# Sums of squares added on VectorE, a constant tile run through TensorE during the first load, and the first eight experts of the first group looked up early

## The reference, cut to what matters

```
y = rmsnorm(h, mix_norm_g[0]);  h = h + mixer_ab(y)         # attention heads and short convolutions
y = rmsnorm(h, ffn_norm_g[i]);  h = h + peer(y)             # both layers
...
rmsnorm: x * rsqrt(mean(x*x) + EPS) * g
peer:    q = y @ w_q                                        # 8 heads x 2 halves x 128
         s = q . sub_keys (128 keys for each half)
         val, idx = top_k(s, 16)                            # for each half
         cand = val0[:, None] + val1[None, :]               # 16 x 16
         top_val, top_pos = top_k(cand, 16);  expert = idx0*128 + idx1 at top_pos
         out = sum_k softmax(top_val)_k * gelu(u[expert_k] . y) * v[expert_k]
```

## Time and profile before

| | |
|---|---|
| median of 3 runs | 1607.42 us (1606.4 to 1611.76) |
| the profiled execution's own time | 1606.77 us |
| its span | 1605.0 us |
| busy: PE, DVE, ACT, POOL | 1046.8, 1111.9, 461.3, 500.8 us |
| DMA | 646.70 MB, mean 403 GB/s |

### The profile page before, as it was taken

How to read it: one execution, slowest core, us unless ns; L and a number is a source line. 1 busy time by engine, 2 the same in 40 slices (tenths; PEclk the granted TensorE clock), 3 DMA queues, 4 the chain that set the end, 5 groups by cost and what they waited for, 6 DMA issues and landing times.

```text
span 1605.0 us, 19986 instructions
## 1 busy us (share of the span) xinstructions
PE 1046.8 (65%) x6936; PEld 711.0 (44%) x6936; DVE 1111.9 (69%) x3119; ACT 461.3 (29%) x953; POOL 500.8 (31%) x541
## 2 busy tenths in 40 slices
PE   8997876757734577778574477877576444544454
PEld 8995642525511266656362155665263111211111
DVE  3436878676457776997756777987765777777764
ACT  4111553111111345742111335743222111111110
POOL 0003333333223333332322323332332333333330
PEclk9998877867955699888796589877788555555666
DMA  9979999999999999999999999999999999999994
GB/s 369 408 259 402 374 420 421 417 421 420 416 420 420 421 378 415 420 415 394 422 416 420 421 411 403 417 405 374 420 418 419 421 422 421 421 421 423 420 420 190
DMA packets 105300, 646.70 MB, mean 403 GB/s; under 512 B 11632, under 2 KB 15728, under 8 KB 37616
## 3 DMA queue, kind: packets, MB, share of 16 engines
q0 software_dynamic: 76032, 553.68, 83.5%
q1 hardware_dynamic: 25536, 89.66, 14.2%
q10 hardware_dynamic: 3632, 2.08, 0.4%
HBM read 644.33 MB, written 1.05 MB: 402 GB/s over the span
## 4 chain that ended last, share of the span: by engine, by line
DMA 40%; PE 28%; DVE 15%; POOL 5%; issue 5%; ACT 4%; DVEq 2%; POOLq 0%; ACTq 0%
DMA ring<-in_uv_dram,expert 36%; PE ps L691 14%; DVE ring L1221 7%; PE ps L868 7%; POOL ring L406 5%; DMA wring<-in_wall_dram 5%; PE ps L881 2%; DVE side L1276 2%; PE ps L698 1%; PE ps L909 1%; ACT side L590 1%; PE ps L856 1%; ACT yg L471 1%; ACT osb L651 1%; ACT L475 0%
## 5 line engine op out<-in xcount | busy, mean ns | idle before, releaser
L1221 DVE CUSTOM_DVE_ANT_0 ring<-ring,ps 128x1024 f32<-128x1024 f32 x528 | 634.8, 1217 | 314.9 <-DMA ring<-in_uv_dram,expert 261.2
L406 POOL DMA_INDIRECT ring<-in_uv_dram,expert x528 | 498.7, 945 | 1068.8 <-PE ps L868 808.2
L868 PE MATMUL ps<-ring,mix 128*32 128x512 f32 x2112 | 369.3, 834 | 327.3 <-DVE mix L1237 327.3
L868 PEld LDWEIGHTS ps<-ring,mix 128*32 128x32 f32 x2112 | 67.8, 135 | 531.7 <-DVE mix L1237 391.0
L665 ACT ACTIVATE gel<-dots 128x4 f32<-128x4 f32 x132 | 27.1, 205 | 761.7 <-DVE dots L1221 761.4
L691 PE MATMUL ps<-yT,wring 128*128 128x128 f32 (+1 forms) x1184 | 159.6, 294 | 48.2 <-DMA wring<-in_wall_dram 27.6
L691 PEld LDWEIGHTS ps<-yT,wring 128*128 128x128 f32 x1184 | 150.7, 202 | 63.6 <-DMA wring<-in_wall_dram 34.2
L881 PE MATMUL ps<-sel,osb 128*128 128x16 f32 x528 | 84.1, 304 | 70.6 <-ACT osb L651 70.6
L881 PEld LDWEIGHTS ps<-sel,osb 128*128 128x128 f32 x528 | 80.7, 241 | 108.9 <-ACT osb L651 108.9
L590 ACT ACTIVATE side<-ident,params 128x128 f32<-128x128 f32 x310 | 96.3, 389 | 15.6 <-PE ps L909 14.8
L856 PE MATMUL ps<-ident,yg 128*128 128x128 f32 x264 | 48.0, 342 | 58.0 <-DVE dots L1221 58.0
(11 more groups left out here) (211 smaller groups left out, 1135.5 us busy)
## 6 DMA issues: line engine op xcount, KB each, us to landing
wring<-in_wall_dram SPq DMA_DIRECT2D x102, 512.0 KB, 11.8
ring<-in_wall_dram SPq DMA_DIRECT2D x44, 512.0 KB, 14.5
kept<-in_wall_dram SPq DMA_DIRECT2D x24, 512.0 KB, 17.0
ring<-in_uv_dram,expert POOLq DMA_INDIRECT x528, 16.1
out_dram<-fo ACTq DMA_DIRECT2D x16, 64.0 KB, 6.7
hT<-in_xT_dram ACTq DMA_DIRECT2D x1, 576.0 KB, 15.9
hT<-in_xT_dram SPq DMA_DIRECT2D x2, 256.0 KB, 3.2
params<-in_smalls_dram ACTq DMA_DIRECT2D x1, 380.0 KB, 17.7
```

The costliest lines, as they stand in the source:

```text
L406: pool.indirect_dma_start(out=ring[:, i % R, :], out_offset=None, in_=uv, in_offset=bass.IndirectOffsetOnAxis(ap=expert[:, n % 2, k:k + 1] ...
L868: mm = pe.matmul(po[32 * j:32 * j + 32, half, :], mix[:, k, :], ring[:, slot, D + 512 * half:D + 512 * (half + 1)], start=(q == 0), stop=( ...
L1221: nc.vector.tensor_tensor_reduce(out=row, in0=row, in1=yrep, scale=1.0, scalar=0.0, op0=ALU.mult, op1=ALU.add, accum_out=dots[:, k:k + 1]) ...
```

## The change

1. *Sums of squares.* VectorE adds the eight squared blocks (one reduction each for part A and xB, seven additions for the second sum), and TensorE needs one matmul with ones in place of eight. The first one stands behind `inA` 0. The reduction of xB stands in VectorE's program behind the evacuation of `inA` 4.
2. *A constant tile.* Before `inA` 0, TensorE runs eight matmuls of `ones` by `ones` into a bank that nobody reads. ScalarE runs a root on the constant `epsc` before it waits for the first sum.
3. *Order on ScalarE.* The loads of xB and of the parameters are issued behind the root of the first norm.
4. *Experts.* The blocks of `qA` (and `qB`) go by halves: blocks 0 to 7 are the first half of all heads. Half 0 of group 0's scores is made after `qA` 9, and VectorE picks its best 16 after the evacuation of `qA` 11. The first eight experts of group 0 are finished, and announced by `s_half`, before the other eight.

```
 [ScalarE]
+            act.wait_ge(s_const, 6)
+            act.activation(warm[:, :], epsc[:, :], ACT.Sqrt)
+            act.wait_ge(s_ss, 1)
+            act.activation(rstd[:, 0:TA], ps[:, 7, 0:TA], ACT.Sqrt, bias=epsc[:, :], scale=1.0 / D).then_inc(s_rms, 1)
             act.dma_start(hT[:, :, TA:L], xT[:, C * TA:C * L].rearrange("p (c t) -> p c t", t=TB)).then_inc(s_x[2], 16)
             act.dma_start(params[:, PAR["conv"]:NPAR], smalls[:, PAR["conv"]:NPAR]).then_inc(s_par2, 16)
-            act.wait_ge(s_const, 6)
-            act.wait_ge(s_ss, 1)
-            act.activation(rstd[:, 0:TA], ps[:, 7, 0:TA], ACT.Sqrt, bias=epsc[:, :], scale=1.0 / D).then_inc(s_rms, 1)
             act.wait_ge(s_x[2], 16)
             act.activation(sqB0[:, :, :], hT[:, :, TA:L], ACT.Square).then_inc(s_sqx, 1)
...
 [TensorE]
             pe.wait_ge(s_const, 6)
-            for c in range(C):
-                pe.wait_ge(s_sq, 2 * c // C + 1)
-                last = pe.matmul(ps[:, 7, 0:TA], ones[:, :], sq[:, c, :], start=(c == 0), stop=(c == C - 1))
-            last.then_inc(s_ss, 1)
+            for _ in range(8):
+                pe.matmul(ps[:, 6, 0:P], ones[:, :], ones[:, :], start=True, stop=True)
             for k in range(24):
                 if k == 0:
                     pe.wait_ge(s_hg, C)
                 chunk("inA", k, lambda c: yT[:, c, 0:TA], TA)
+                if k == 0:
+                    pe.wait_ge(s_sum, 1)
+                    pe.matmul(ps[:, 7, 0:TA], ones[:, :], rs[:, 0:TA], start=True, stop=True).then_inc(s_ss, 1)
...
-            pe.wait_ge(s_sqx, 1)
+            pe.wait_ge(s_sumx, 1)
             pe.wait_ge(s_ze, 2)
-            for c in range(C):
-                last = pe.matmul(ps[:, 3, 0:TB], ones[:, :], sqB0[:, c, :], start=(c == 0), stop=(c == C - 1))
-            last.then_inc(s_ssx, 1)
+            pe.matmul(ps[:, 3, 0:TB], ones[:, :], xs[:, 0:TB], start=True, stop=True).then_inc(s_ssx, 1)
...
             for k in range(C):
                 chunk("outA", k, lambda c: mixT[:, c, 0:TA], TA)
-                if k >= 2:
-                    second_sums(k - 2)
...
                 chunk("qA", k, lambda c: hg2[:, c, :], TA)
                 if k == 0:
-                    second_sums(C - 2)
-                    second_sums(C - 1)
+                    pe.wait_ge(s_sum, 2)
+                    pe.matmul(ps[:, 7, 0:TA], ones[:, :], rs[:, 0:TA], start=True, stop=True).then_inc(s_ss, 1)
+                if k == 9:
+                    evacuated(pe, "qA", 6)
+                    evacuated(pe, "qA", 7)
+                    pe.wait_ge(s_par2, 16)
+                    score(0, 0).then_inc(s_sc0, 1)
...
 [VectorE]
+            dve.wait_ge(s_sq, 2)
+            nc.vector.tensor_reduce(out=rs[:, 0:TA], in_=sq[:, :, :].rearrange("p c t -> p t c"), axis=AX, op=ALU.add
+                                    ).then_inc(s_sum, 1)
...
+                if k == 4:
+                    dve.wait_ge(s_sqx, 1)
+                    nc.vector.tensor_reduce(out=xs[:, 0:TB], in_=sqB0[:, :, :].rearrange("p c t -> p t c"), axis=AX, op=ALU.add
+                                            ).then_inc(s_sumx, 1)
...
+            def add_square(c):
+                dve.wait_ge(s_sq2, c + 1)
+                if c > 1:
+                    dve.wait_ge(s_add, c - 1)
+                return nc.vector.tensor_tensor(rs[:, 0:TA], sq[:, 0, :] if c == 1 else rs[:, 0:TA], sq[:, c, :], ALU.add)
...
                 nc.vector.tensor_scalar(hg2[:, c, :], hv, par("ffn_g", c), None, ALU.mult).then_inc(s_hg2, 1)
+                if c >= 2:
+                    add_square(c - 1).then_inc(s_add, 1)
...
             last.then_inc(s_yx, 1)
+            add_square(C - 1).then_inc(s_sum, 1)
...
+                if k == 11:
+                    best_half(0, s_sc0)
...
+            def route_first():
+                spare = rest[:, :, :].rearrange("p s (k j) -> p s k j", j=TOPK)
+                best_pairs(0)
+                dve.drain()
+                nc.vector.max_index(topp[:, 0:8], topv[:, 0:8], c1)
+                rows_of(0, slice(0, 8), spare).then_inc(s_half, 1)
+                nc.vector.match_replace(c2, topv[:, 0:8], c1, LOW)
+                nc.vector.tensor_scalar(negm[:, :], topv[:, 0:1], -1.0, None, ALU.mult)
+                dve.drain()
+                nc.vector.max(topv[:, 8:16], c2).then_inc(s_top, 1)
+                dve.drain()
+                nc.vector.max_index(topp[:, 8:16], topv[:, 8:16], c2)
+                rows_of(0, slice(8, 16), spare).then_inc(s_idx, 1)
...
-            route_best(0)
-            route_pairs(0)
-            route_experts(0)
+            best_half(1, s_sc)
+            route_first()
             route_best(1)
...
 [GpSimd]
+            pool.wait_ge(s_half, 1)
             for n in range(N):
-                pool.wait_ge(s_idx, n + 1)
                 for k in range(TOPK):
+                    if k == 0 and n or k == 8 and n == 0:
+                        pool.wait_ge(s_idx, n + 1)
```

More of the change, by code:

```diff
@@ L201, in hybrid_trunk @@
         xs = sb("xs", [P, BW])
+        warm = sb("warm", [P, 1])
         rs = sb("rs", [P, BW])
@@ L535, in front @@
                             act.wait_ge(s_sc, GF)
-                        act.copy(qT[:, k % 2, :, k // 2, :], ps[:, m % 2, 0:TB].rearrange("p (g t) -> p g t", t=GT)
+                        act.copy(qT[:, k // H, :, k % H, :], ps[:, m % 2, 0:TB].rearrange("p (g t) -> p g t", t=GT)
                                  ).then_inc(s_bank[m % 2], 1)
@@ L763, in _, with score @@
                 chunk("outA", k, lambda c: mixT[:, c, 0:TA], TA)
-                if k >= 2:
-                    second_sums(k - 2)
+            def score(n, s):
+                return pe.matmul(psc[:, s * NK:(s + 1) * NK], qT[:, s, query(n), :, :].rearrange("p h t -> p (h t)"),
+                                 keysT[:, 2 * layer_of(n) + s, :], start=True, stop=True)
             for k in range(16):
@@ L845, in scores @@
                     pe.wait_ge(s_psc, n)
-                for s in range(2):
-                    last = pe.matmul(psc[:, s * NK:(s + 1) * NK], qT[:, s, query(n), :, :].rearrange("p h t -> p (h t)"),
-                                     keysT[:, 2 * layer_of(n) + s, :], start=True, stop=True)
+                for s in range(2) if n else (1,):
+                    last = score(n, s)
                 last.then_inc(s_sc, 1)
@@ L1005, in log_weights, with best_half @@
                                                ).then_inc(s_lw, 1)
+            sc = [psc[:, s * NK:(s + 1) * NK] for s in range(2)]
+            cand = pairs[:, 0, :, :]
+            c1, c2 = (pairs[:, i, :, :].rearrange("p a b -> p (a b)") for i in range(2))
+            hot = pairs
+            def best_half(s, ready):
+                dve.wait_ge(ready, 1)
+                nc.vector.max(val[:, s, 0:8], sc[s])
+                dve.drain()
+                nc.vector.max_index(idx[:, s, 0:8], val[:, s, 0:8], sc[s])
+                last = nc.vector.match_replace(rest[:, s, :], val[:, s, 0:8], sc[s], LOW)
+                if s == 1:
+                    last.then_inc(s_psc, 1)
+                dve.drain()
+                nc.vector.max(val[:, s, 8:16], rest[:, s, :])
@@ new lines, in route_best @@
+            def route_best(n):
+                dve.wait_ge(s_sc, n + 1)
+                for s in range(2):
+                    nc.vector.max(val[:, s, 0:8], sc[s])
+                dve.drain()
+                for s in range(2):
+                    nc.vector.max_index(idx[:, s, 0:8], val[:, s, 0:8], sc[s])
+                    last = nc.vector.match_replace(rest[:, s, :], val[:, s, 0:8], sc[s], LOW)
+                last.then_inc(s_psc, 1)
+                dve.drain()
+                for s in range(2):
+                    nc.vector.max(val[:, s, 8:16], rest[:, s, :])
@@ new lines, in best_pairs @@
+            def best_pairs(n):
+                dve.drain()
+                for s in range(2):
+                    nc.vector.max_index(idx[:, s, 8:16], val[:, s, 8:16], rest[:, s, :])
+                nc.vector.tensor_tensor(cand, val[:, 0, :].unsqueeze(2).to_broadcast([P, TOPK, TOPK]),
+                                        val[:, 1, :].unsqueeze(1).to_broadcast([P, TOPK, TOPK]), ALU.add)
+                dve.drain()
+                nc.vector.max(topv[:, 0:8], c1)
+                nc.vector.tensor_scalar(idxf[:, 0, :], idx[:, 0, :], float(NK), None, ALU.mult)
+                nc.vector.tensor_scalar(idxf[:, 1, :], idx[:, 1, :], float(layer_of(n) * NE), None, ALU.add)
@@ new lines, in rows_of @@
+            def rows_of(n, ks, hot):
+                count = ks.stop - ks.start
+                dve.drain()
+                nc.vector.tensor_scalar(posu[:, 0, ks], topp[:, ks], 4, None, ALU.logical_shift_right)
+                nc.vector.tensor_scalar(posu[:, 1, ks], topp[:, ks], 15, None, ALU.bitwise_and)
+                dve.drain()
+                nc.vector.tensor_copy(posf[:, :, ks], posu[:, :, ks])
+                dve.drain()
```

(14 more changed lines are left out.)

45 lines of the change are left out of this document (21 added, 24 removed).

## The result

The changed kernel is slower: 1617.1 us median of 6 runs (1615.84 to 1621.56) against 1608.07 us (6 runs), ratio 1.0057, 95% interval 1.0045 to 1.007, or +9.2 us (7.2 to 11.3). The forecast was +6.6 us and 1614.0, with a range from 1603.5 to 1619.

What follows compares the result with a forecast made beforehand. TensorE's program up to 138 us was taken as the bound, moving the end one for one. Stall +6.9, restart +2.0, start +1.0, sums -1.72, -1.34, -0.22 gave +6.6 on 1607.42: 1614.0 us, range 1603.5 to 1619.

Steps and rivals of the forecast that it cites:

- The bound: TensorE's program up to 138 us: what moves its end of `inB` 15 moves the indirect loads and the end one for one.
- the loads decide: Rival: the DMA engines, busy from 120 us, set the end, so the earlier first load counts: +3.0, 1610.4 us; chance 0.08.
- Part 1, the start: At the start, `inA` 0 begins at about 7.75 us, only 0.25 sooner, awaiting weights; +1.0 us in the sum.
- Half pace: TensorE at half pace through `inA` 0 and the first sum costs 0 to 1.9 us more; 1.0 taken.
- Part 2, the load of xB: Load issued at 9.95 lands at 25.9; VectorE waits for its square, so TensorE's block 7 is late: +6.9 us.
- The slow restart: Behind the gap before block 7, TensorE at half pace for 3.0 to 4.4 us loses 1.5 to 2.2; 2.0 taken.
- Part 3, the other sums: Fewer TensorE matmuls for L751 and the second sums: -1.72, -1.34 and -0.22 us; VectorE's additions covered.
- Part 4, the experts: Loads of group 0 can begin some 3.6 us sooner against TensorE, filling an idle stretch; priced at nothing.
- The sum: Whole kernel: +6.9 + 2.0 + 1.0 - 1.72 - 1.34 - 0.22 = +6.6 us, for a median of 1614.0 us.
- the held-up issue: Rival: ScalarE's issue of xB stands behind SyncE's in a full queue, stall 1.4 to 2.7 us longer: 1617 us; chance 0.15.
- The rule beside the row: The Trainium skill's DMA queue turns by packets of 9 to 17 descriptors, against single records; would act like the short landing.
- the short landing: Rival: queues share by bytes, xB lands at 17.9 and the stall is gone: -3.7, 1603.7 us; chance 0.08.

Runs made afterwards that it cites:

- e1: The changed kernel with ScalarE's loads of xB and the parameters back in their early place; ratio to the kernel before 0.9999, 1607.9 us.
- e3: The kernel before with only the loads of xB and the parameters moved behind the root; ratio to the kernel before 1.0005.
- e4: The changed kernel without the eight matmuls on the constant tile; ratio to the kernel before 1.0054.
- e2: The changed kernel, load still late, with VectorE's reduction of xB moved from behind `inA` 4 to behind `inA` 20; ratio to the kernel before 1.0002.
- e8: e5 with GpSimd waiting for all 16 experts of group 0 before its first load; ratio to the kernel before 1.0015, median 1616.40 us.
- e5: The changed kernel with the load of xB issued early and its reduction behind `inA` 20; ratio to the kernel before 1.0004, median 1616.76 us.
- e6: e5 with 13 matmuls on the constant tile in place of 8; ratio to the kernel before 0.9996.
- e9: e5 with the start as before: no constant tile, no root on a constant, first sum by eight matmuls; ratio to the kernel before 0.9994.
- e12: e6 repeated unaltered; ratio to the kernel before 0.9987.
- e11: The kernel before, repeated unaltered as a control; ratio 0.9993.

## Why the prediction was right, and where its sizes were off

*The bound, and that the end follows TensorE's front.* Right for large steps. The front of 138.58 us moved by 10.4 us in the changed kernel, the load behind the hole by 11.0, and the median by 9.2 (ratio times 1608, interval 7.2 to 11.3). e1 to e3, whose fronts are +0.9, -0.9 and +0.2 us, lie within 0.8 us of no change by their ratios, and within 2.3 by their intervals. For steps of one or two microseconds the measurement can't tell: from the front to the load behind the hole it takes 52.5 us before and 53.0 to 53.7 in the profiles after and of e1 to e4. The rival that the loads decide falls with e2 (see e8).

*Part 1, the start.* Right that the eight sums hid behind the first weights: `inA` 0 waited for them at 8.05. I had said 7.75; it began between 7.46 and 8.53 in the runs without the eight sums. Half pace, of which I took 1.0 us out of 0 to 1.9, was the full 1.9 here. The table shows a spread for which no row gives a reason: with eight constant matmuls and 1.6 to 2.3 us of nothing behind them, two of six profiles had full pace (behind gaps of 1.7 and 1.8 us; the one behind 1.6 us had half pace); with thirteen both; with none neither.

*Part 2, the load of xB.* The mechanism was right, link by link, and e1, e2 and e3 show that it takes both the late load and the early wait. VectorE waited 9.79 us for ScalarE's square, and TensorE stood for 8.14 us (7.5 forecast). The size was too small. `inA` 7 began at 32.62 against 21.9, +10.7 us, where the sum has 6.9 and the 1.0 of the slow start. The missing 2.8 are: 0.3 from the first weights, 0.9 from the pace, 0.8 from the landing (16.7 for 15.9), and 0.8 from the reduction. The last is the term that was mis-sized by a wrong row: I carried 512 adjacent elements in 0.69 us on at 1 ns each, and the reduction of 1152 elements, each 144 elements from the next it is added to, took 2.09, about 1.8 ns each. The trace before had nearer rows, two reductions over views with the added elements apart, of 128 and of 64 elements a partition:

```profile
5.55 0.36 DVE L976 TENSOR_REDUCE sel<-ident 128x16 f32<-128x128 f32 x1
5.83 0.25 DVE L978 TENSOR_REDUCE sel<-ident 128x16 f32<-128x64 f32 x1
```

64 elements more cost 0.11 us, 1.7 ns each, and carried on to 1152 elements that gives 2.1 us. The slow restart cost 2.5 us for 2.0.

*Part 3, the other sums.* -3.28 was forecast. From +10.7 + 2.5 = 13.2 us behind the restart to +10.4 at the copy are -2.8; half a microsecond stays behind, 0.24 of it as the issue row at 69.98. Another 0.2 was never to be had: the sixth of the sums behind `outA` had run while TensorE waited for VectorE anyway (0.6 us before, 0.8 after). VectorE's additions are hidden, as said.

*Part 4, the experts.* Right: 2.9 us sooner against TensorE, and not seen at the end. The first load came at 122.86 where 118 was forecast, since TensorE's delay was larger.

*The sum.* +10.7 + 2.5 - 2.8 = +10.4 against +6.6, and +9.2 by the ratio. All terms of the delay were too small, and none made up for another. The result lies above the forecast's own range (1612 to 1616), on the 1617 of the rival with the held-up issue. That this rival gives the number is luck: ScalarE's issue took 0.39 us as before, and from issue to landing it was 16.6 to 16.9 us in the five profiles with the late issue, and 15.7 to 17.8 in the nine with the early one.

*The rule beside the row.* The prediction lets turns by bundles shorten the landing. They would not by themselves: bundles with as many records from either queue also serve them one for one. Only a sharing by bytes gives the short landing, and after the change too the records say otherwise (from 17 to 27 us 931 and 932, 3.40 and 0.54 MB).

*A faster version* was looked for in e5, e6, e9 and e12. Their copies behind `inB` 15 (137.91 to 138.91) are 0.8 to 1.8 us sooner than e11's 139.74, and their ratios, 0.9987 to 1.0004, include 1 each time. None is shown to be faster.

## What to carry to other kernels

A wait put into the program of an engine that evacuates for another can be as dear as the latest thing it may wait for: 8.1 us of TensorE here. Ask for each new wait what is queued behind it, and place it where its answer has long been there: moving one reduction from block 4 to block 20 was worth 8 to 9 us here (e2 against e4 and the changed kernel). And before work is taken off the start of a path, look at what lands next: the eight matmuls that were done while the first weights were on their way cost next to nothing (`inA` 0 began at 8.22 with them and at 8.05 without), and `inA` 0 and 1 behind them were at full pace (e9: 32 records in 3.88 us).

## What was not expected of the hardware

- Reductions of VectorE over a strided view: 1024 elements a partition in 1.87 us, 1152 in 2.09, against 512 adjacent ones in 0.69 (1.8 against 1.35 ns an element, fixed part included). The reductions differ in the distance of the elements and in how many make one sum (8 against 16), and no run parts the two.
- A load of 576 KB in records of 576 bytes took 15.7 to 17.8 us to land beside the weights when it was issued at about 4.7 us, and 16.6 to 16.9 when issued at 8.3 to 12.4: no effect of the other queue's fill is seen.
- Running TensorE for 3.6 to 3.8 us and then leaving it 1.6 to 2.3 us without work gave full pace in two of six profiles, and something between in two more.
